# Second attention: the transposes of a pair's probabilities in the middle of the filling chunk, not ahead of it

## The chip, the cores and the metric

The kernel runs on one core of one Trainium2 chip. The metric is the device time of one execution in microseconds (us), the median of several executions. The engines are named as in the profile: PE is TensorE (its matmuls), PEld its weight loads, DVE is VectorE, ACT is ScalarE, POOL is GpSimd, SP issues most of the weight transfers.

## The reference

Two transformer blocks follow each other on 256 tokens of width 1024, in float32. The change lies in the second block, in its two attentions (one with a forget gate, "F", and one with three branches: selected blocks "S", window "W", compressed "C"). Cut to what matters:

```
z = rms_norm(x, norm_mix) @ w_in
y_a = rg_lru_mixer(...)            # recurrence: gelu(gate) * scan
y_b = short_conv_mixer(...)        # three taps
y_c = fox_mixer(...)               # 4 heads: softmax(q k + decay) v           "F"
y_d = nsa_mixer(...)               # 4 heads: g0*softmax_c v + g1*softmax_s v + g2*softmax_w v
mixed = concatenate([rms_norm(y_a), rms_norm(y_b), rms_norm(y_c), rms_norm(y_d)])
x = x + mixed @ w_out
```

That makes 16 jobs (head and branch), each a score, a softmax, a transpose of the probabilities and a product with the values.

## The kernel before

Every engine has an instruction stream written by hand, and they meet in semaphores; nothing is scheduled automatically. A float32 matrix product is made of three matmuls on split operands (`product`, L1949 to L1951: high times high, high times low, low times high). Weights arrive by DMA in `raw`, ACT writes the high part `w_hi` (L719) and DVE the low part `w_lo` (L1246); this runs four panels ahead of PE.

The 16 jobs of the second attention are taken two at a time: pairs 0 to 7, of kinds F, F, S, W, C, S, W, C. For pair x (loop over `PAIRS`, jobs a and b) the streams do this:

- PE: `make_scores` of pair x+1 (L2188 and L2189, for kind C L2185 and L2186); `turn(a)`, `turn(b)`: transposes of pair x's probabilities into banks ps2 and ps3 (L2202, three each, for kind C L2199, two each); for pairs 0 to 6 one chunk of the input projection, `chunk_out`, 8 products of three matmuls, "the filling chunk"; for pair 7 instead `wout_panel(0)`, the first panel of the output projection, as long as a chunk; then `gather(a)`, `gather(b)`: products with the values (L2224 and L2225, for kind C L2218).
- DVE: scores of pair x+1 out of the banks (L1461, L1464), a weight split, sometimes a piece of the recurrence or convolution, then the probabilities of pair x+1, scaled by L1483, which raises `p_ready`. `turn` waits for `p_ready`.
- ACT, in this order: exponentials of job a+2 (L897), `pt_copy(a)` and `pt_copy(b)` (L907, for kind C L905): copies of the transposes to `ptb`, which raise `pt_copied`; exponentials of job b+2; then the copy of the filling chunk (L1070). `pt_copy` waits for the transposes (`pt_done`), `gather` for `pt_copied`.

After pair 7 ACT goes on with the Gelu of the recurrence's gate (L1200, with an activation table load ahead of it), the squares of y_b (L1149), a second table load (L1203), the root of their row sum (L1154) and the squares of y_a (L1149). DVE answers with L1740 (sum of two squares, `y_tot`), the scan L1815, L1818 (`ya_ready`), L1744, L1749 (scaled y) and L1756 (its low part, `y_lo`). PE answers in `y_sums(1)` (L2035) and `y_spread(1)` (L2055). `wout_panel(n)` waits for `y_lo` to reach n+1, so `wout_panel(0)` waits for the first L1756 of `y_low(0)`, which DVE does behind the probabilities of pair 7, and `wout_panel(2)` for the first L1756 of `y_low(1)`. `y_sums(1)` stands between `gather` of pair 7 and `wout_panel(1)`, and waits for `y_tot`.

Of the kernel before, what the change touches and what calls it, by code (L numbers as in the profile page):

```python
# [21 lines left out]
KC = D // P  # L22
# [53 lines left out]
FILL_AT = {0: 3, 1: 4, 2: 5, 3: 6, 4: 7, 5: 8, 6: 9}  # L76
# [56 lines left out]
def build(nc, I, out):  # L133
# [111 lines left out]
    def nth(name, k=0):  # L245
        return order[at[name]] + k

    ctx = ExitStack()
    with ctx:
# [39 lines left out]
        def take(*shape, rows=P, start=None):  # L289

            if start is not None:
                where[0] = start
            n = int(np.prod(shape))
            v = arena[0:rows, where[0]:where[0] + n]
            where[0] += n
            assert where[0] <= ARENA, where
            names = "abcd"[:len(shape)]
            if len(shape) > 1:
                v = v.rearrange("p (%s) -> p %s" % (" ".join(names), " ".join(names)),
                                **dict(zip(names[1:], shape[1:])))  # L300
            return v
# [16 lines left out]
        ang, turns, arg = (take(TT, HALF) for _ in range(3))  # L318
# [83 lines left out]
        def s(name):  # L402
            if name not in S:
                S[name] = sem(name)
            return S[name]
# [91 lines left out]
        L = {}  # L497
# [30 lines left out]
        def lin(l, n=SEQ, a=0):  # L528
            return LIN[l % 2][:, a:a + n]
# [9 lines left out]
        def free_name(l):  # L539
            return "lin_free%d" % (l % 2)  # L540
# [50 lines left out]
        def z_buf(g):  # L591

            return (zs if (g // 2) % 2 != (N1 // 2) % 2 else zb)[:, g % 2, :]

        def turned(g):

            if g % 2 == 0:
                return ps[2][:, 0:FW]
            return ps[3][:, 0:FW] if g >= N1 else ps[6][:, P:P + FW]
# [5 lines left out]
        def hi_lo(m, a, n):  # L605
            return w_hi[:, m % HL, a:a + n], w_lo[:, m % HL, a:a + n]
# [18 lines left out]
        for n, (_, parts) in enumerate(panels):  # L625
            raised[n % RAW] += 16 * (len(parts) if parts else 1)
            raw_count.append(raised[n % RAW])
# [1314 lines left out]
        def _(pe):  # L1942
# [3 lines left out]
            def product(dst, stat, mov, start, stop, shared=False):  # L1946

                kw = {"skip_group_check": True} if shared else {}
                T.matmul(dst, stat[0], mov[0], start=start, stop=False, **kw)  # L1949
                T.matmul(dst, stat[0], mov[1], start=False, stop=False, **kw)  # L1950
                return T.matmul(dst, stat[1], mov[0], start=False, stop=stop, **kw)  # L1951
# [4 lines left out]
            def mxp(c):  # L1956
                return mix_hi[:, c, :], mix_lo[:, c, :]

            def await_split(m, i=0):
                pe.wait_ge(lo_done, m + 1 + i * 6)  # L1960

            def await_bank(l):

                if l >= 2:
                    name, v = freed[l - 2]
                    pe.wait_ge(s(name), v)

            def chunk_out(l, act, fresh=None, order=range(KC), middle=None):


                m = outputs[l]
                await_split(m)
                await_bank(l)
                for n, k in enumerate(order):
                    if fresh is not None:
                        pe.wait_ge(s(fresh[0]), fresh[1] + n + 1)
                    if middle is not None and n == KC // 2:
                        middle()
                    ins = product(lin(l), hi_lo(m, k * P, P), act(k), n == 0, n == KC - 1)
                ins.then_inc(panel_used, 1)  # L1980
# [46 lines left out]
            for b in range(4):  # L2027
                for q in range(4):
                    c, t = 2 * b + q // 2, q % 2
# [22 lines left out]
            def spread(dst, v):  # L2052

                for t in range(TT):
                    ins = T.transpose(dst[:, t * P:(t + 1) * P], v[:, t:t + 1].to_broadcast([P, P]), ident[:, :])  # L2055
                return ins
# [111 lines left out]
            def make_scores(g):  # L2168
                kind, h = ALL[g]
                if g >= 2:  # L2170
                    pe.wait_ge(s("z_ready"), g - 1)
                r = slice(HD * (h % 2), HD * (h % 2) + HD)
                if kind == "A":
                    q, k = aqT[r, h // 2, :], akT[r, h // 2, :]
                elif kind == "M":
                    pe.wait_ge(s("qk_copied"), h + 1)
                    q, k = [qkb[:, 2 * x:2 * x + 2, :].rearrange("p a b -> p (a b)") for x in range(2)]
                elif kind == "F":
                    q, k = fqT[r, h // 2, :], fkT[r, h // 2, :]
                else:  # L2180
                    q = nqT[r, h // 2, :]
                    own, other = kskw[r, :], kskw_x[r, :]
                    k = {"S": (own, other)[h % 2], "W": (other, own)[h % 2], "C": kcT[r, :]}[kind]
                if kind == "C":
                    T.matmul(ps[g % 2][:, 0:NCMP0], q[:, 0:P], k[:, 0:NCMP0], start=True, stop=True)  # L2185
                    ins = T.matmul(ps[g % 2][:, P:P + NCMP], q[:, P:SEQ], k[:, 0:NCMP], start=True, stop=True)  # L2186
                else:
                    T.matmul(ps[g % 2][:, 0:P], q[:, 0:P], k[:, 0:P], start=True, stop=True)  # L2188
                    ins = T.matmul(ps[g % 2][:, P:FW], q[:, P:SEQ], k[:, 0:SEQ], start=True, stop=True)  # L2189
                line(ins, "s_done")  # L2190

            def turn(g):

                pe.wait_ge(s("p_ready"), 2 * (g + 1))
                if g >= 2:
                    pe.wait_ge(s("pt_copied"), g - 1)
                if ALL[g][0] == "C":
                    for t in range(TT):
                        ins = T.transpose(turned(g)[0:NCMP, t * P:(t + 1) * P], zc[:, g % 2, t, 0:NCMP], ident[:, :])  # L2199
                else:  # L2200
                    for b in range(3):
                        ins = T.transpose(turned(g)[:, b * P:(b + 1) * P], z_buf(g)[:, b * P:(b + 1) * P], ident[:, :])  # L2202
                line(ins, "pt_done")
# [29 lines left out]
            for x in range(NP1):  # L2233
                a, b = 2 * x, 2 * x + 1
# [189 lines left out]
            for kv in range(2):  # L2424
                for half in range(2):
                    m = ADA + 2 * kv + half
                    n = direct_of[m]
# [59 lines left out]
            def y_sums(n):  # L2487

                pe.wait_ge(s("y_tot"), n + 1)
                if n >= 1:  # L2490
                    pe.wait_ge(s("y_rms"), n)
                    pe.wait_ge(s("y_ready"), 2)
                line(by_token(YSUM[:, 2 * n:2 * n + 2], sq[:, Y_SQ[n], :]), "y_ss")

            def y_spread(n):

                pe.wait_ge(s("y_inv"), n + 1)
                line(spread(Y_FAC[n], yrms[:, 2 * n:2 * n + 2]), "y_fac")

            def wout_panel(n, middle=None):  # L2500

                m, k = nth("wout", n), Y_ROWS[n]
                await_split(m)
                pe.wait_ge(s("y_lo"), n + 1)
                if n == 0:
                    for l in L["fill"][8:10]:
                        pe.wait_ge(s(free_name(l)), freed[l][1])
                for c in range(KC):
                    if c == KC // 2 and middle is not None:
                        y_spread(middle)  # L2510
                    ins = product(ACC2[c // 2][:, SEQ * (c % 2):SEQ * (c % 2) + SEQ], hi_lo(m, c * P, P), mxp(k),
                                  n == 0 and c % 2 == 0, False, shared=True)
                ins.then_inc(panel_used, 1)
# [19 lines left out]
            for x, (a, b) in enumerate(PAIRS):  # L2533
                if x + 1 < len(PAIRS):
                    if x == 1:
                        pe.wait_ge(s("qk_ready"), 7)
                    for g in (a + 2, b + 2):
                        if ALL[g] == ("S", 1):
                            pe.wait_ge(s("kskw_x_in"), 32)
                        if ALL[g] == ("C", 0):  # L2540
                            pe.wait_ge(s("kc_ready"), 1)
                            pe.wait_ge(s("vc_ready"), 1)
                        make_scores(g)
                turn(a)
                turn(b)
                if x in FILL_AT:
                    chunk_out(L["fill"][FILL_AT[x]], hx)
                if x == len(PAIRS) - 1:
                    wout_panel(0)
                gather(a)  # L2550
                gather(b)
                if x == 3:
                    y_sums(0)
                if x == 5:
                    y_spread(0)
# [53 lines left out]
```

## Time and profile before

| | us |
|---|---|
| median of 3 runs | 751.49 |
| lowest and highest of them | 751.16 and 754.23 |
| the profiled execution | 751.95 |
| its span, first to last instruction | 750.1 |
| PE busy in it | 718.8 (96%) |
| DVE busy in it | 549.2 (73%) |
| ACT busy in it | 448.9 (60%) |
| mean granted clock of PE | 0.995 |

A span is the time between the first and the last instruction of the core; 1.85 us of the profiled execution lie around it. A granted clock of 1.00 is 2.4 GHz, 0.50 is 1.2 GHz. The stretch of the second attention is 485 to 536 us from the span's start.

### The profile page before, as it was taken

Reading aid. Unit: us, or ns where it says so; the run is one execution under the profiler, and the core shown is the slowest. Engines: PE = TensorE matmul, PEld = TensorE weight load, DVE = VectorE, ACT = ScalarE, POOL = GpSimd, SP = SyncE. Lnnn points to the kernel's source line nnn. Section 1 sums busy time; section 2 is a strip of 40 time slices with the busy share of each in tenths; the row PEclk is TensorE's granted clock in tenths of the full one; section 3 lists DMA queues with packets and bytes.
Section 4 is the critical chain, followed back from the end, with each engine's and each line's share of the span. In section 5 each row is a group of like instructions: output and inputs, shape, how many; then the busy total and the mean of one; then the engine's idle time right before and its main releaser. Section 6 shows DMA issues by size and latency. Waiting matters only on the chain.

```text
span 750.1 us, 13966 instructions
## 1 busy us (share of the span) xinstructions
PE 718.8 (96%) x4944; PEld 647.4 (86%) x4944; DVE 549.2 (73%) x1060; ACT 448.9 (60%) x857; POOL 78.1 (10%) x112
## 2 busy tenths in 40 slices
PE   2799999999999999999999999999999999999998
PEld 2699898899999899999999999877898888888886
DVE  4887459898797786666666678887887876776764
ACT  5667466666655655455554577898657554545552
POOL 8003021000356000000000002600000000000000
PEclk9999999999999999999999999999999999999999
DMA  9997798888799367665666748842155865666531
GB/s 289 354 289 239 190 218 255 279 270 261 227 333 261 110 188 212 188 194 169 181 199 185 162 117 210 222 139 91 41 158 169 239 181 174 195 192 192 169 112 57
DMA packets 187237, 148.37 MB, mean 198 GB/s; under 512 B 13681, under 2 KB 171315, under 8 KB 187177
## 3 DMA queue, kind: packets, MB, share of 16 engines
q1 hardware_dynamic: 183296, 143.61, 64.8%
q10 hardware_dynamic: 2232, 3.03, 2.2%
q0 software_dynamic: 1664, 1.15, 0.8%
q8 instruction: 27, 0.44, 0.2%
q14 instruction: 18, 0.14, 0.0%
HBM read 146.44 MB, written 1.36 MB: 197 GB/s over the span
## 4 chain that ended last, share of the span: by engine, by line
PE 83%; DVE 7%; ACT 5%; DMA 2%; issue 2%; POOL 0%; SPq 0%; DVEq 0%; ACTq 0%; POOLq 0%
PE ps L2334 20%; PE ps L1949 15%; PE ps L1951 14%; PE ps L1950 14%; PE ps L2336 10%; DMA raw<-in_w_ada 2%; DVE w_lo L1246 2%; DVE arena L1304 1%; ACT w_hi L719 1%; PE ps L2311 1%; PE ps L1997 1%; PE ps L2224 1%; PE ps L2202 1%; PE ps L2189 1%; PE ps L2188 1%
## 5 line engine op out<-in xcount | busy, mean ns | idle before, releaser
L1246 DVE TENSOR_TENSOR w_lo<-raw,w_hi 128x1024 fp32r<-128x1024 f32 (+3 forms) x223 | 270.6, 1235 | 66.7 <-ACT w_hi L719 65.5
L719 ACT ACTIVATE w_hi<-raw 128x1024 fp32r<-128x1024 f32 (+3 forms) x223 | 226.0, 1038 | 22.3 <-DMA raw<-in_w_in 7.8
L2334 PE MATMUL ps<-h,w_hi 128*128 128x512 f32 x672 | 239.1, 396 | 0.0
L2336 PE MATMUL ps<-h,w_lo 128*128 128x256 f32 x672 | 189.4, 282 | 0.0
L2334 PEld LDWEIGHTS ps<-h,w_hi 128*128 128x128 f32 x672 | 126.3, 188 | 29.5
L1949 PE MATMUL ps<-h,w_hi 128*128 128x256 f32 (+1 forms) x440 | 126.9, 288 | 3.7 <-DVE h L1323 1.9
L2336 PEld LDWEIGHTS ps<-h,w_lo 128*128 128x128 f32 x672 | 126.2, 188 | 1.0
L1951 PE MATMUL ps<-h,w_lo 128*128 128x256 f32 (+1 forms) x440 | 123.6, 281 | 0.0
L1950 PE MATMUL ps<-h,w_hi 128*128 128x256 f32 (+1 forms) x440 | 123.5, 281 | 0.0
L1949 PEld LDWEIGHTS ps<-h,w_hi 128*128 128x128 f32 (+1 forms) x440 | 82.7, 188 | 7.7 <-issue 5.0
L1950 PEld LDWEIGHTS ps<-h,w_hi 128*128 128x128 f32 (+1 forms) x440 | 82.8, 188 | 0.0
L1951 PEld LDWEIGHTS ps<-h,w_lo 128*128 128x128 f32 (+1 forms) x440 | 82.6, 188 | 0.1
L998 ACT ACTIVATE arena<-ps 128x256 f32<-128x256 f32 x44 | 16.8, 382 | 70.4 <-PE ps L2336 69.4
L1949 PE MATMUL ps<-g_hi,w_hi 128*128 128x256 f32 x176 | 49.3, 280 | 0.0
L1950 PE MATMUL ps<-g_lo,w_hi 128*128 128x256 f32 x176 | 49.2, 280 | 0.0
L1951 PE MATMUL ps<-g_hi,w_lo 128*128 128x256 f32 x176 | 49.2, 279 | 0.0
L1949 PE MATMUL ps<-mix_hi,w_hi 128*128 128x256 f32 x160 | 47.2, 295 | 1.2 <-DVE mix_lo L1756 0.6
L1011 ACT ACTIVATE g_hi<-arena 128x256 fp32r<-128x256 f32 x44 | 18.4, 418 | 47.3 <-DVE arena L1608 47.3
L1950 PE MATMUL ps<-mix_lo,w_hi 128*128 128x256 f32 x160 | 45.1, 282 | 0.0
L1951 PE MATMUL ps<-mix_hi,w_lo 128*128 128x256 f32 x160 | 45.1, 282 | 0.0
L1588 DVE TENSOR_TENSOR arena<-arena,ps 128x256 f32<-128x256 f32 x44 | 18.5, 420 | 31.7 <-ACT arena L998 31.6
L1007 ACT ACTIVATE arena<-ps 128x256 f32<-128x256 f32 x44 | 16.9, 384 | 40.6 <-PE ps L2336 40.6
(380 smaller groups left out, 1248.3 us busy)
## 6 DMA issues: line engine op xcount, KB each, us to landing
raw<-in_w_in SPq DMA_DIRECT2D x53, 512.0 KB, 5.7
raw<-in_w_down SPq DMA_DIRECT2D x44, 512.0 KB, 4.3
raw<-in_w_gate_up SPq DMA_DIRECT2D x44, 512.0 KB, 4.5
raw<-in_w_ada SPq DMA_DIRECT2D x32, 512.0 KB, 5.0
raw<-in_w_gate SPq DMA_DIRECT2D x22, 512.0 KB, 4.0
raw<-in_w_up SPq DMA_DIRECT2D x22, 512.0 KB, 5.0
raw<-in_w_ada SPq DMA_DIRECT2D x32, 256.0 KB, 6.7
raw<-in_w_o SPq DMA_DIRECT2D x8, 512.0 KB, 5.2
```

The costliest lines, as they stand in the source:

```text
L719: A(w_hi[:, m % HL, 0:w], raw[:, n % RAW, 0:w], ACT.Copy).then_inc(hi_done, 1)
L998: line(A(g_part[:, j % 2, :], bank_of(f, j)[:, SEQ:512], ACT.Copy), "g_part")
L1007: line(A(u_part[:, j % 2, :], UP[j % 2][:, SEQ:512], ACT.Copy), "u_part")
L1011: line(A(g_hi[:, j % 2, :], hf[:, j % 2, :], ACT.Copy), "g_hi")
L1246: V.tensor_tensor(w_lo[:, m % HL, 0:w], raw[:, n % RAW, 0:w], w_hi[:, m % HL, 0:w].bitcast(f32), sub).then_inc(lo_done, 1)
L1304: ins = stt(out=dst, in0=src, scalar=cond[:, k:k + 1], in1=dst, op0=mult, op1=add)
L1588: line(V.tensor_tensor(g_all[:, j % 2, :], g_part[:, j % 2, :], bank_of(f, j)[:, 0:SEQ], add), "g_sum")
L1949: T.matmul(dst, stat[0], mov[0], start=start, stop=False, **kw)
L1950: T.matmul(dst, stat[0], mov[1], start=False, stop=False, **kw)
L1951: return T.matmul(dst, stat[1], mov[0], start=False, stop=stop, **kw)
L2334: T.matmul(bank[:, :], hi, h2[:, k, :, :].rearrange("p a b -> p (a b)"), start=(k == 0), stop=False, skip_group_check=True)
L2336: ins = T.matmul(bank[:, 0:SEQ], lo, h_hi[:, k, :], start=False, stop=(k == KC - 1), skip_group_check=True)
```

## The change

`wout_panel` and `chunk_out` take a function that is called in the middle of their eight products. The two turns of a pair are handed over to it, for pairs 0 to 6 in the filling chunk and for pair 7 in the first output panel, where they stood ahead of both. Nothing else differs; only PE's order changes.

```diff
-            def wout_panel(n, middle=None):
+            def wout_panel(n, middle=None, between=None):
...
                 for c in range(KC):
                     if c == KC // 2 and middle is not None:
                         y_spread(middle)
+                    if c == KC // 2 and between is not None:
+                        between()
                     ins = product(ACC2[c // 2][:, SEQ * (c % 2):SEQ * (c % 2) + SEQ], hi_lo(m, c * P, P), mxp(k),
                                   n == 0 and c % 2 == 0, False, shared=True)
...
                         make_scores(g)
-                turn(a)
-                turn(b)
+
+                def turns():
+
+                    turn(a)
+                    turn(b)
                 if x in FILL_AT:
-                    chunk_out(L["fill"][FILL_AT[x]], hx)
+                    chunk_out(L["fill"][FILL_AT[x]], hx, middle=turns)
                 if x == len(PAIRS) - 1:
-                    wout_panel(0)
+                    wout_panel(0, between=turns)
                 gather(a)
                 gather(b)
```

PE at pair 1, before: scores of pair 2 into ps0 and ps1, then the transposes of pair 1 (`sq` holds the probabilities), then the chunk (`h2` are the activations). The semaphores on which a row waits stand behind it.

```order
L2188 MATMUL ps0<-arena 128x128 [waits z_ready,qk_ready]
L2189 MATMUL ps0<-arena 128x256
L2188 MATMUL ps1<-arena 128x128 [waits z_ready,kskw_x_in]
L2189 MATMUL ps1<-arena 128x256
L2202 MATMUL ps2<-ident,sq 128x128 [waits pt_copied,p_ready]
L2202 MATMUL ps2<-ident,sq 128x128 x2
L2202 MATMUL ps3<-ident,sq 128x128 [waits pt_copied,p_ready]
L2202 MATMUL ps3<-ident,sq 128x128 x2
L1949 MATMUL ps4<-h2,w_hi 128x256 [waits lru_sig,lo_done]
```

The same place in the changed program:

```order
L2188 MATMUL ps1<-arena 128x128 [waits z_ready,kskw_x_in]
L2189 MATMUL ps1<-arena 128x256
L1949 MATMUL ps4<-h2,w_hi 128x256 [waits lru_sig,lo_done]
...
L2202 MATMUL ps2<-ident,sq 128x128 [waits pt_copied,p_ready]
L2202 MATMUL ps2<-ident,sq 128x128 x2
L2202 MATMUL ps3<-ident,sq 128x128 [waits pt_copied,p_ready]
L2202 MATMUL ps3<-ident,sq 128x128 x2
L1949 MATMUL ps4<-h2,w_hi 128x256
```

Twelve matmuls of the chunk now stand ahead of the six transposes and twelve behind them. Pairs 0 and 2 to 6 look alike.

PE at pair 7, before: the last `gather` of pair 6 into ps7, the transposes of pair 7 (`zc`), the first output panel (24 matmuls from `mix_hi` and `mix_lo`), `gather` of pair 7 and `y_sums(1)`.

```order
L2225 MATMUL ps7<-ptb,arena 64x128
L2199 MATMUL ps2<-ident,zc 15x128 [waits pt_copied,p_ready]
L2199 MATMUL ps2<-ident,zc 15x128
L2199 MATMUL ps3<-ident,zc 15x128 [waits pt_copied,p_ready]
L2199 MATMUL ps3<-ident,zc 15x128
L1949 MATMUL ps0<-mix_hi,w_hi 128x256 [waits lin_free0,lin_free1,y_lo,lo_done]
...
L2218 MATMUL ps7<-ptb,arena 64x256 [waits pt_copied] x2
L2035 MATMUL ps6<-ones,sq 128x1 [waits y_ready,y_rms,y_tot]
```

The same place in the changed program:

```order
L2225 MATMUL ps7<-ptb,arena 64x128
L1949 MATMUL ps0<-mix_hi,w_hi 128x256 [waits lin_free0,lin_free1,y_lo,lo_done]
...
L2199 MATMUL ps2<-ident,zc 15x128 [waits pt_copied,p_ready]
L2199 MATMUL ps2<-ident,zc 15x128
L2199 MATMUL ps3<-ident,zc 15x128 [waits pt_copied,p_ready]
L2199 MATMUL ps3<-ident,zc 15x128
L1949 MATMUL ps4<-mix_hi,w_hi 128x256
...
L2218 MATMUL ps7<-ptb,arena 64x256 [waits pt_copied] x2
```

Here the transposes moved behind a wait for `y_lo` and twelve matmuls. DVE, ACT and SP have the same order in both programs, and so do POOL's instructions of this stretch.

## Rows read from the trace of the kernel before

**Rows 1.** PE's waits over the whole span: total us, times, longest us.

```profile
PE ps L2224 <- ACT ptb L907: 1.4, 1, 1.4
...
PE ps L1949 <- DVE mix_lo L1756: 0.6, 1, 0.6
```

**Rows 2.** Timeline of PE at pair 1: start, duration; idle before and releaser in brackets.

```profile
495.47 1.20 PE L2202 MATMUL ps<-ident,sq 128*128 128x128 f32 x6 [1.24 <-DVE sq L1483]
496.43 0.36 PE L1949 MATMUL ps<-h,w_hi 128*128 128x256 f32 x1
...
499.43 0.66 PE L2224 MATMUL ps<-ptb,arena 128*64 128x256 f32 x4
...
500.24 0.50 PE L2188 MATMUL ps<-arena 64*128 64x128 f32 x4
```

**Rows 3.** Timeline of PE, an earlier chunk that is already cut in the middle.

```profile
476.20 0.39 PE L1949 MATMUL ps<-h,w_hi 128*128 128x256 f32 x1
...
477.72 0.38 PE L2440 MATMUL ps<-ident,arena 128*128 128x128 f32 x2
```

**Rows 4.** Timeline of DVE at pair 1: job b's probabilities.

```profile
495.52 0.55 DVE L1483 TENSOR_SCALAR sq<-sq,small 128x128 f32<-128x128 f32 x2
```

**Rows 5.** Timeline of ACT: the copies to ptb of pairs 0, 1 and 5.

```profile
490.81 0.87 ACT L907 ACTIVATE ptb<-ps 128x384 f32<-128x384 f32 x2
...
497.75 0.85 ACT L907 ACTIVATE ptb<-ps 128x384 f32<-128x384 f32 x2
...
521.39 0.85 ACT L907 ACTIVATE ptb<-ps 128x384 f32<-128x384 f32 x2
```

**Rows 6.** Timeline of PE at pair 7 and the output panels behind it.

```profile
528.24 0.52 PE L2225 MATMUL ps<-ptb,arena 128*64 128x128 f32 x3
529.86 0.39 PE L2199 MATMUL ps<-ident,zc 128*15 128x128 f32 x2 [1.11 <-DVE zc L1483]
530.93 0.59 PE L2199 MATMUL ps<-ident,zc 128*15 128x128 f32 x2 [0.68 <-DVE zc L1483]
531.30 0.55 PE L1949 MATMUL ps<-mix_hi,w_hi 128*128 128x256 f32 x1
...
534.00 0.41 PE L1949 MATMUL ps<-mix_hi,w_hi 128*128 128x256 f32 x1
...
535.69 0.65 PE L2218 MATMUL ps<-ptb,arena 15*64 15x256 f32 x4
...
536.26 0.61 PE L2035 MATMUL ps<-ones,sq 128*128 128x1 f32 x4
...
540.19 0.35 PE L1949 MATMUL ps<-mix_hi,w_hi 128*128 128x256 f32 x1
```

**Rows 7.** Windows: length, busy us (instructions) of PE, PEld, DVE, ACT, POOL; granted clock, DMA.

```profile
495.00:500.00 5.00, 4.42 (x36) 3.92 (x38) 4.75 (x23) 4.86 (x15) 0.00 (x0) 1.00 0.43 123
...
530.80:531.00 0.20, 0.07 (x1) 0.07 (x2) 0.20 (x2) 0.00 (x0) 0.00 (x0) 0.95 1.13 343
...
534.20:534.50 0.30, 0.30 (x4) 0.30 (x3) 0.30 (x1) 0.30 (x2) 0.00 (x0) 0.68 0.00 0
```

**Rows 8.** Timeline of ACT behind pair 7.

```profile
531.56 0.37 ACT L905 ACTIVATE ptb<-ps 15x256 f32<-15x256 f32 x1 [0.90 <-PE ps L2199]
531.95 1.28 ACT L1200 ACT_TABLE_LOAD   x1
533.25 0.63 ACT L1200 ACTIVATE arena<-arena 128x512 f32<-128x512 f32 x1
534.14 0.72 ACT L1149 ACTIVATE sq<-bias 128x256 f32<-128x256 f32 x2 [0.26 <-DVE bias L1808]
```

**Rows 9.** Timeline of DVE behind pair 7.

```profile
530.78 0.76 DVE L1756 TENSOR_TENSOR mix_lo<-bias,mix_hi 128x256 fp32r<-128x256 f32 x2
...
534.89 0.43 DVE L1740 TENSOR_TENSOR sq<-sq 128x256 f32<-128x256 f32 x1 [0.19 <-ACT sq L1149]
...
539.62 0.82 DVE L1756 TENSOR_TENSOR mix_lo<-bias,mix_hi 128x256 fp32r<-128x256 f32 x2
```

## The prediction

> **What bounds the kernel now.** I read the page first: PE is busy for 96% of the span, so a moved instruction can only gain where PE stands idle. PE's waits show how little that is: in and behind the second attention 1.24 us at pair 1's transposes, 1.4 us at pair 5's products with the values, 1.11 and 0.68 us at pair 7's transposes, 0.6 us late in the output projection [rows 1, 2, 6]. The reader is to see two kinds of wait there. Those for DVE L1483 (probabilities not ready) are what a later place for the transposes can cover. The one for ACT L907 is the reverse: the copy of the transposes was late, and later transposes can't help it. Then I read the timelines of PE, DVE and ACT side by side over 485 to 560 us, and the chain of waits through it: up to pair 1 it runs through ACT and DVE, in pairs 2 to 4 through PE, from pair 5 to pair 7 through ACT and DVE again.
>
> **Pair 1, a gain.** PE was done with the last scores at 495.47 − 1.24 = 494.23 and stood there until job a's probabilities came; job b's came at 495.52 + 0.55 = 496.07 [rows 2, 4]. Turns of pair 1 and their waiting held PE until 496.43. Changed, the first half of the chunk fills this. It takes 1.52 us, the length of the half that is cut already [rows 3], so from 494.2 to 495.7; turn(b) can start at 496.2 (0.06 us for the semaphore, and some 0.1 us because pair 0's copy, before at 490.81 [rows 5], comes a little later behind its half chunk); it is over by 496.6 and the second half by 498.1. Before, the gather began at 499.43 [rows 2]. Not all of these 1.3 us are kept: ACT's copies of pair 1 stand behind exponentials that DVE sets, so they stay at 497.75, 0.85 us for the two [rows 5], and 0.1 us of delay: job b's is there at 498.7. So gather(b) starts at about 498.8, takes half of the 0.81 us from 499.43 to 500.24 [rows 2], and the next scores start at 499.2, where they stood at 500.24: **1.05 us earlier**.
>
> **Pairs 0 and 2 to 6, nothing or a little loss.** Work only changes places. Two cut halves of 1.52 us are 3.04, a whole chunk is 3.00 [rows 2, 3]: 0.04 us a pair for the extra change of operands, on the path in pairs 2, 3 and 4 and partly inside other waits: **0.05 us lost** is my value for the three, 0.25 us the other end. The cover for the copies shrinks from a whole chunk to half; two copies take 0.87 us [rows 5], with semaphores some 1.1, so 1.5 us hold them if ACT is free, and in its timeline ACT waits for scores in pairs 2 to 4. If it doesn't hold, each of these pairs loses up to 0.5 us. In pair 5 the wait stays: ACT's course there begins at the end of pair 4's chunk and passes two table loads before it copies at 521.39 [rows 5]. All of that shifts with PE, so the 1.0 us goes through pair 5, and through DVE's queue up to pair 7.
>
> **Pair 7, a loss.** Here the half panel can't fill the wait, as it waits itself: for `y_lo`, which DVE raises behind the same probabilities. The first L1756 ends at about 531.2, some 0.4 us after its start at 530.78 [rows 9]; PE began the panel at 531.30 with the transposes done inside the wait [rows 6]. Changed, all is 1.0 us earlier by pair 1: the panel begins at 530.25. PE then has been idle since 527.8, 2.5 us in one piece. Before it was 2.2 us (528.76 to 530.93) with the first two transposes in between, and the granted clock fell from 1.00 to 0.50, 2.4 to 1.2 GHz, at about 530.95 and rose at about 534.3 [rows 7]. I take the same fall, for 3.3 us. Twelve matmuls of the panel took 534.00 − 531.30 = 2.70 us at 0.50 [rows 6], where a half at 1.00 is 1.52. So the first half ends at 532.95; turn(a) takes 0.37 us as turn(b) did (530.93 to 531.30 [rows 6]); turn(b) starts at 533.3; the second half takes 1.5 us at the full clock and ends at 535.2. Before, the gather began at 535.69 [rows 6]: PE is still 0.5 us ahead.
>
> ACT is not. It copied job b 0.63 us after the start of turn(b), in 0.37 us, and the table load for the Gelu followed at 531.95 [rows 6, 8]. Now that is 533.3 + 0.63 + 0.37 + 0.02 = 534.3, **2.35 us later**. The Gelu ends at 536.2 where it ended at 533.9. The squares behind it had waited 0.26 us for DVE [rows 8], which is done by then, so they and all that hangs on them come 2.1 us later: DVE's sum L1740 ends at 537.4 in place of 535.3 [rows 9]. `y_sums(1)` then starts at 537.4, not at 536.26 [rows 6]: PE, ready for it at 535.75, stands for 1.7 us. The sums and panel 1 take 3.93 us (536.26 to 540.19 [rows 6]), until 541.4; panel 2 needs the first half of `y_low(1)`, before at 539.62 + 0.41 = 540.03 [rows 9], 0.16 us ahead of PE, now at 542.1. PE starts panel 2 at 542.2, **2.0 us later** than before. Behind it DVE and ACT are driven by PE, the wait for mix_lo [rows 1] shifts with them, and the feed-forward part is PE's alone, so nothing gives this back.
>
> Two rules of the Trainium skill bear on this. The delay rests on ACT keeping its order: in rows 8 it idles 0.90 us for L2199 while the Gelu, whose input is there, stands behind. "PSUM — Partial Sum Buffer", Engine vs sequencer instructions, says the same, that ScalarE's and VectorE's queues are strictly first in, first out; without that rule the Gelu would keep its place and the result would be 1.0 us less than before, with it 2.0 more. On the clock, rows 7 give one fall of 3.3 us. "TensorE: Matmul & The Clock Gate", What's actually happening, says that the number of slow matmuls after a pause varies from run to run of one kernel; by the row the first half panel costs 2.70 us, by the page it may cost as little as at the full clock.
>
> **The sum.** −1.05 + 0.05 = −1.0 us up to pair 7, and 3.0 us lost from there to panel 2, make +2.0 us. The profiled execution's own time is 751.95 us (span 750.1), so it would be 753.9; it stands 0.46 us above the median of 751.49, so the forecast for the median is **753.5 us**. A measurement of this kernel tells about 0.5%, 3.8 us, from no change: I forecast a small loss that counts as the same.
>
> **The rivals.**
> - *The clock doesn't fall, or only after the first half panel.* For it: the wait of 1.24 us at pair 1 left it at 1.00 [rows 7]. Against: PE is idle longer here than when it fell. Then the half takes 1.52 us, turn(b) starts at 531.9, the table load comes 1.0, the squares 0.7 and panel 2 0.6 us later: 752.1 us. (This is also what the page on the clock would allow.) Chance 0.13.
> - *The delay at pair 7 is absorbed and pair 1's gain stays* (the other side). The table load is on time if turn(b) starts by 530.93, which decides. For it: at the full clock PE needs no more than `y_lo` by 529.2, a gain ahead of pair 7 of 2.0 us. Against: the gain is 1.0, and DVE's and ACT's work from pair 5 on has no idle that could shrink so far. 750.5 us. Chance 0.10, of it 0.02 for a gain of over 0.5%, which would take three quarters of all waits named above.
> - *Slower: the new wait of 1.7 us ahead of `y_sums(1)`, so soon after the pause of 2.5 us, brings or keeps the clock at 0.50.* Panel 1 at 0.50 takes 2 × (2.70 − 1.52) = 2.3 us more, of which 0.6 lie in the wait for `y_lo`: 755.2 us. Half a panel more at 0.50, 1.2 us, or late copies in pairs 2 to 4, 0.5 us each, take it over 755.25. For it: the clock fell at a like mixture of idle and work [rows 6, 7]. Against: it didn't in pair 1. Chance 0.16.
> - *No effect*, because turns and chunk are the same work: 751.5 us, chance 0.03. Against it, rows 8: copies and Gelu follow the turns directly.
>
> **How the numbers follow.** The forecast has 0.58, with its own range of 752.7 to 754.3 (0.25 us for the cuts, 0.7 us for where the clock rises). With the rivals at 750.5 and 752.1 below and 755.2 above, a range from 750.9 to 755.5 leaves out the gain case and the worst of the clock case, some 0.15. Slower by over 0.5% takes the part of the third rival beyond 755.25, and a median drawn up as the one run of 754.23 before was: 0.12. Faster by over 0.5%: 0.02. Within: 0.86.
>
> **What the profile after would show.** Right: no wait of L2202 at pair 1; the distance from DVE's last L1483 of pair 7 to the table load L1200 grown by about 3.3 us; a new wait of PE at L2035 for L1740 of 1 to 2 us, one of about 0.6 us at L1949 for L1756 at panel 2; a clock of 0.50 over most of the first half of panel 0. Wrong in the loop: waits at L2224 in pairs 2 to 4 of over 0.2 us each. The prediction fails if panel 0 begins well ahead of 530 us, if the clock stays at 1.00, or if L1200 isn't late.

## The result, and the profile after

The changed kernel takes **753.95 us** (median of 20 executions, 752.12 to 755.95) against 751.58 us (median of 20, 750.82 to 754.51) of the kernel before in the same session. The two medians lie 2.4 us apart. The ratio taken from all executions is 1.0027 (that of the medians alone would be 1.0032), 95% interval 1.0017 to 1.0038, so +2.0 us (+1.3 to +2.9): a small loss, within 0.5%. The profiled execution took 754.01 us, its span is 752.1 us, the mean granted clock 0.995 as before.

PE's work is the same. Busy times of the page after:

```profile
PE 719.0 (96%) x4944; PEld 647.7 (86%) x4944; DVE 548.8 (73%) x1060; ACT 448.2 (60%) x857; POOL 76.1 (10%) x112
```

Its waits moved. PE's waits after, over the whole span (total us, times, longest us); the first two answer to [rows 1]:

```profile
PE ps L1949 <- DVE mix_lo L1756: 3.6, 3, 2.5
...
PE ps L2224 <- ACT ptb L907: 1.7, 2, 1.5
...
PE ps L2035 <- DVE sq L1740: 0.7, 1, 0.7
```

Three waits for `mix_lo` stand where there was one of 0.6 us: 2.5 us ahead of panel 0, 0.35 ahead of panel 2, and the old one. The wait of `y_sums(1)` is new. The one for L2202 at pair 1 is gone. L2224 waits twice, 1.5 us in pair 5 (1.4 before) and 0.2 us in pair 1; nowhere in pairs 2 to 4.

Timeline of PE after, pair 1, answering to [rows 2] (start, duration, idle before and releaser). L2485 in the first row is the last work ahead of the pairs; the two programs are the same up to it:

```profile
486.53 1.97 PE L2485 MATMUL ps<-bias,arena 128*128 128x256 f32 x8
...
496.10 1.09 PE L2202 MATMUL ps<-ident,sq 128*128 128x128 f32 x6
...
498.79 0.81 PE L2224 MATMUL ps<-ptb,arena 128*64 128x256 f32 x3 [0.19 <-ACT ptb L907]
...
499.44 0.38 PE L2224 MATMUL ps<-ptb,arena 128*64 128x256 f32 x1
...
499.96 0.50 PE L2188 MATMUL ps<-arena 64*128 64x128 f32 x4
```

The transposes no longer wait. Timeline of PE after, pair 7 and the output panels, answering to [rows 6]:

```profile
531.08 0.36 PE L1949 MATMUL ps<-mix_hi,w_hi 128*128 128x256 f32 x1 [2.55 <-DVE mix_lo L1756]
...
532.92 1.05 PE L2199 MATMUL ps<-ident,zc 128*15 128x128 f32 x4
533.63 0.56 PE L1949 MATMUL ps<-mix_hi,w_hi 128*128 128x256 f32 x1
...
536.08 0.65 PE L2218 MATMUL ps<-ptb,arena 15*64 15x256 f32 x4
...
537.45 0.61 PE L2035 MATMUL ps<-ones,sq 128*128 128x1 f32 x4 [0.72 <-DVE sq L1740]
...
542.09 0.36 PE L1949 MATMUL ps<-mix_hi,w_hi 128*128 128x256 f32 x1 [0.35 <-DVE mix_lo L1756]
```

The waits of 1.11 and 0.68 us at the two turns [rows 6] are one of 2.55 us now, ahead of panel 0; two further ones follow, ahead of `y_sums(1)` and of panel 2. Timeline of ACT after, behind pair 7, answering to [rows 8]:

```profile
533.58 0.80 ACT L905 ACTIVATE ptb<-ps 15x256 f32<-15x256 f32 x2 [4.51 <-PE ps L2199]
534.40 1.28 ACT L1200 ACT_TABLE_LOAD   x1
535.70 0.63 ACT L1200 ACTIVATE arena<-arena 128x512 f32<-128x512 f32 x1
536.23 0.70 ACT L1149 ACTIVATE sq<-bias 128x256 f32<-128x256 f32 x2
```

ACT stands for 4.51 us for the turns, and the Gelu, whose input is there, stands behind. The 0.26 us that the squares had waited for DVE are gone. Granted clock around panel 0, by windows of PE (length, busy us (instructions), clock, DMA share, GB/s), answering to [rows 7]:

```profile
531.50:532.00 0.50, 0.50 (x7) 1.00 0.17 48
532.00:532.50 0.50, 0.50 (x6) 0.64 0.00 0
...
535.50:536.00 0.50, 0.50 (x5) 0.95 0.00 0
```

Here it fell some 1 us after the panel's start (from the third quarter of the first half on) and stood at 0.50 until about 535.5. Before, it fell ahead of the panel's start.

Since L2485 starts at another time in every profile (484.9 to 490.1 us, from code that is the same in all), everything below is told as the **distance from its start**. "End" is the end of the span, at the last instruction. In the profile before it starts at 486.10:

```profile
486.10 1.97 PE L2485 MATMUL ps<-bias,arena 128*128 128x256 f32 x8
```

| distance, us | panel 0 | Gelu's table load | `y_sums(1)` | panel 2 | end |
|---|---|---|---|---|---|
| before | 45.20 | 45.85 | 50.16 | 54.09 | 264.00 |
| after | 44.55 | 47.87 | 50.92 | 55.56 | 265.57 |
| change | −0.65 | +2.02 | +0.76 | +1.47 | +1.57 |

What moves L2485 lies ahead of everything that was changed, and it is a good part of the scatter of the times: over the profiles L2485 moves by 5.2 us, the distance from it to the end by 2.8. Between 80 and 118 us ACT waits for weights. These are its waits in the profile before (total us, times, longest us):

```profile
ACT w_hi L719 <- DMA raw<-in_w_in: 2.4, 2, 2.0
```

And these in that of e1, the run below whose L2485 starts last, at 490.11:

```profile
ACT w_hi L719 <- DMA raw<-in_w_in: 7.4, 3, 5.6
```

In the three profiles with L2485 behind 488.9 (e1, e2, e6) PE then waits for ACT L889 near 115 us for 2.4 to 3.6 us, and the granted clock is 0.50 for some microseconds behind it. In all others, with L2485 at 484.9 to 486.8, this wait is 0.9 to 1.7 us and the clock stays at 1.00 there. The sum of ACT's waits isn't the measure (4.8 us in e12, whose L2485 starts at 485.21); what in the transfers brings the long wait about wasn't followed.

### The profile page after: what moved, and what is told of

It reads as the page before. It is cut to its first block, busy times and chain, and to the rows that moved or that the text cites. A ratio compares the mean times of both kernels' runs of the same rounds, so it can differ in the third digit from the quotient of the medians.

```text
span 752.1 us, 13966 instructions
## 1 busy us (share of the span) xinstructions
PE 719.0 (96%) x4944; PEld 647.7 (86%) x4944; DVE 548.8 (73%) x1060; ACT 448.2 (60%) x857; POOL 76.1 (10%) x112
## 4 chain that ended last, share of the span: by engine, by line
PE 80%; ACT 6%; DVE 5%; DMA 5%; issue 2%; SPq 0%; POOL 0%; ACTq 0%; DVEq 0%; POOLq 0%
PE ps L2334 20%; PE ps L1949 14%; PE ps L1951 13%; PE ps L1950 13%; PE ps L2336 10%; DMA raw<-in_w_in 3%; DMA raw<-in_w_ada 2%; ACT w_hi L719 2%; DVE w_lo L1246 2%; PE ps L2311 1%; PE ps L1997 1%; PE ps L2224 1%; DVE arena L1304 1%; PE ps L2189 1%; PE ps L2202 1%
```

## The experiments

The theory was the one on record: pair 1 gains, pair 7 loses more, through the place of the Gelu behind the copies in ACT's order. The rivals were that the loss comes from the clock alone, from the cuts of the other pairs, or that the half panel ahead of the turns matters in itself. Distances of all profiles, in us, and the times; e1 to e4 ran on one chip, e5 to e8 on a second, e9 to e12 on a third. The clock column names a fall close to the pairs' end. Three programs were profiled twice (before and e9, after and e10, e3 and e11): their distances to panel 0 agree within 0.06 us, those to panel 2 within 0.18, 0.69 and 0.00 us. The 0.69 goes with a fall of the clock in one of the two. From panel 2 to the end all profiles lie within 0.4 us (209.9 to 210.3), so smaller differences at the end say nothing. In e6 the panel begins with the turns, and the distance is theirs.

| | turns in the middle for | panel 0 | table load | `y_sums(1)` | panel 2 | end | clock there | ratio to before, interval |
|---|---|---|---|---|---|---|---|---|
| before | none | 45.20 | 45.85 | 50.16 | 54.09 | 264.00 | falls | |
| e9 before again | none | 45.20 | 45.64 | 49.26 | 53.91 | 264.17 | stays | single execution, 751.65 us |
| after | all | 44.55 | 47.87 | 50.92 | 55.56 | 265.57 | falls | 1.0027 (1.0017 to 1.0038) |
| e10 after again | all | 44.61 | 47.17 | 50.22 | 54.87 | 265.09 | stays | single execution, 752.27 us |
| e1 | pairs 0 to 6 | 44.61 | 45.06 | 48.68 | 53.33 | 263.39 | falls early | 1.0014 (0.9991 to 1.0038) |
| e2 | pair 7 | 45.20 | 48.22 | 51.27 | 55.92 | 265.97 | falls | 1.0054 (1.0029 to 1.0080) |
| e3 | pair 1 | 44.41 | 44.86 | 48.48 | 53.12 | 263.24 | stays | 0.9992 (0.9972 to 1.0012) |
| e8 | pairs 0, 2 to 6 | 45.39 | 45.84 | 50.49 | 54.42 | 264.51 | falls | 1.0008 (0.9998 to 1.0018) |
| e4 | all, Gelu first | 44.67 | 43.28 | 48.74 | 53.38 | 263.57 | falls early | 1.0007 (0.9987 to 1.0028) |
| e7 | pairs 0 to 6, Gelu first | 44.67 | 42.67 | 48.74 | 53.38 | 263.62 | stays | 0.9998 (0.9987 to 1.0010) |
| e5 | all, PE kept busy | 44.57 | 47.08 | 50.13 | 55.65 | 265.98 | falls late | 1.0022 (1.0001 to 1.0042) |
| e6 | all, pair 7 at 0 products | 44.67 | 45.74 | 48.80 | 53.44 | 263.37 | stays | 0.9991 (0.9980 to 1.0003) |
| e12 | all, pair 7 at 2 products | 44.61 | 46.94 | 50.16 | 54.64 | 264.79 | falls | single execution, 751.90 us |
| e11 | pair 1 | 44.41 | 44.86 | 48.47 | 53.12 | 263.19 | stays | 0.9981 (0.9969 to 0.9993) |

**e1, e2, e3, e8: each part of the change alone.** One condition was put in, and only it differs between the four:

```diff
+                inside = x < len(PAIRS) - 1      # e1; e2: x == len(PAIRS) - 1
+                if not inside:                   # e3: x == 1; e8: x not in (1, len(PAIRS) - 1)
+                    turns()
                 if x in FILL_AT:
-                    chunk_out(L["fill"][FILL_AT[x]], hx, middle=turns)
+                    chunk_out(L["fill"][FILL_AT[x]], hx, middle=turns if inside else None)
                 if x == len(PAIRS) - 1:
-                    wout_panel(0, between=turns)
+                    wout_panel(0, between=turns if inside else None)
```

> Turns in the middle for pairs 0 to 6, ahead of the panel for pair 7 as before. My theory (pair 1 gains, pair 7 loses): the distance from PE's L2485 to the start of panel 2, 54.1 us before and 55.6 us after the change, becomes 53.4; the time is 0.65 us under before, 750.9. Rival, every cut chunk costs and pair 7 costs nothing: the distance stays near 55.6 and the time 2 us above before. Rival, it is all in the clock's fall: it falls here as well, 54 to 55.6 at random.

> Turns in the middle for pair 7 alone. My theory: the whole loss and none of the gain, a distance from L2485 to panel 2 of 56.2 us, 2.1 us over before's 54.1, and a time of 753.7; the table load for the Gelu starts 4 us behind DVE's last L1483, where it was 1.1 before. Rival, cut chunks cost: 54.1 to 54.3 us and no change of time.

> Turns in the middle for pair 1 alone. My theory: the same gain as with pairs 0 to 6, a distance of 53.3 to 53.4 us, since the other pairs' turns never waited. Rival, the cover of each pair adds up: only a part of what pairs 0 to 6 give.

> Turns in the middle for pairs 0 and 2 to 6, ahead in pairs 1 and 7: the price of the cuts alone. My theory: a distance of 54.1 to 54.3 us, 0 to 0.2 over before, time 751.6. Rival, cuts or late copies cost 0.5 us a pair: 55 or more.

Timeline of PE in e2, the start of L2485, then panel 0, `y_sums(1)` and panel 2:

```profile
488.93 1.97 PE L2485 MATMUL ps<-bias,arena 128*128 128x256 f32 x8
...
534.13 0.35 PE L1949 MATMUL ps<-mix_hi,w_hi 128*128 128x256 f32 x1 [2.55 <-DVE mix_lo L1756]
...
540.20 0.61 PE L2035 MATMUL ps<-ones,sq 128*128 128x1 f32 x4 [0.47 <-DVE sq L1740]
...
544.85 0.36 PE L1949 MATMUL ps<-mix_hi,w_hi 128*128 128x256 f32 x1 [0.35 <-DVE mix_lo L1756]
```

Pair 7 alone begins panel 0 where before began it (534.13 − 488.93 = 45.20), has the three waits of the changed kernel, and starts panel 2 at 544.85 − 488.93 = 55.92, 1.83 us late. The loss needs nothing of the loop. The time of e2 came out higher than the 2.2 us that were expected, 4.1 us above before (2.2 to 6.0) from 8 executions, twice what its distance gives. On that chip the times of the kernel before alone run from 751.46 to 757.58 us, and e2's profile has the long wait near 115 us; whether that is all of the surplus isn't shown. Timeline of PE in e3, pair 1 and panel 2:

```profile
485.06 1.97 PE L2485 MATMUL ps<-bias,arena 128*128 128x256 f32 x8
...
494.59 1.04 PE L2202 MATMUL ps<-ident,sq 128*128 128x128 f32 x6
...
497.24 0.81 PE L2224 MATMUL ps<-ptb,arena 128*64 128x256 f32 x3 [0.19 <-ACT ptb L907]
...
498.40 0.50 PE L2188 MATMUL ps<-arena 64*128 64x128 f32 x4
...
538.18 0.35 PE L1949 MATMUL ps<-mix_hi,w_hi 128*128 128x256 f32 x1 [0.35 <-DVE mix_lo L1756]
```

Pair 1 alone has the next scores at 498.40 − 485.06 = 13.34, where before has 14.14 (500.24 [rows 2] less 486.10): 0.80 us, and 0.79 of it is still there at panel 0. So the whole gain of the loop is pair 1's; at panel 2 it is 53.12, a little more than the 53.3 to 53.4 expected. e8 starts panel 0 0.19 us later than before, e1 0.20 later than e3: two comparisons give the cuts of the other six pairs the same price. At panel 2 e1 is still 0.21 behind e3, but e8 is 0.33 behind before, over the 0 to 0.2 that were expected. Its clock fell 0.2 us behind the start of panel 0, in the profile before 0.3 us ahead of it, so that part isn't laid to the cuts.

Half of that price lies at pair 1. Timelines of ACT, DVE and PE in e8 from pair 0's copies to pair 1's transposes (L2485 starts at 485.19):

```profile
490.00 0.88 ACT L907 ACTIVATE ptb<-ps 128x384 f32<-128x384 f32 x2
...
491.64 1.05 ACT L719 ACTIVATE w_hi<-raw 128x1024 fp32r<-128x1024 f32 x1
```

```profile
492.72 1.23 DVE L1246 TENSOR_TENSOR w_lo<-raw,w_hi 128x1024 fp32r<-128x1024 f32 x1 [1.39 <-ACT w_hi L719]
...
494.06 0.55 DVE L1483 TENSOR_SCALAR sq<-sq,small 128x128 f32<-128x128 f32 x2
```

```profile
494.66 1.21 PE L2202 MATMUL ps<-ident,sq 128*128 128x128 f32 x6 [1.33 <-DVE sq L1483]
```

Pair 0's copies begin at a distance of 4.81, before at 490.81 − 486.10 = 4.71 [rows 5]. ACT's next weight split follows them in its order, DVE's low part waits for it with the probabilities behind, and PE's wait is 1.33 us in place of 1.24 [rows 2]: 0.10 us from end to end. The rows also point at what makes PE wait at pair 1 at all: DVE idles 1.39 us for a weight split just ahead of the probabilities. Moving that split wasn't tried.

The times of e1 and e3 on the first chip tell neither from no change; e1's profile alone spent 4 us more ahead of L2485, where it is the same program. What is said of e1 and e3 rests on the distances.

**e4, e7: the Gelu ahead of pair 7's copies.** Only ACT's order differs from the changed kernel (e4) or from e1 (e7); line numbers behind it grow by one:

```diff
+                if not more:
+                    line(A(lg, lg, ACT.Gelu_apprx_tanh), "lg_ready")
                 pt_copy(a)
...
-            line(A(lg, lg, ACT.Gelu_apprx_tanh), "lg_ready")
             act.wait_ge(s("yb_ready"), 1)
```

> The changed kernel, and on ACT the Gelu of the recurrence's gate, with its table load, ahead of pair 7's two copies in place of behind them. My theory (the loss is the Gelu's chain held behind the copies): the squares of y_b start 1.8 us earlier than after the change, PE doesn't wait at y_sums(1), panel 2 starts 1.5 us earlier, distance 54.1 and time as before, 751.5. Rival, the loss is PE's own (the slow clock, the half panel and the turns on its path): panel 2 stays at 55.6 us and the time at 753.9.

> Pairs 0 to 6 in the middle, pair 7 ahead of the panel, and the Gelu ahead of pair 7's copies: the version that the theory points to. The squares of y_b then wait for DVE alone; behind pair 7 PE itself is next. Distance 53.3 to 53.4 us, time 750.7 to 750.9, no better than without the Gelu's move by more than 0.2 us. Rival, ACT still bounds there: another 0.5 us or more off.

Timeline of ACT in e4 behind pair 7:

```profile
529.01 1.28 ACT L1178 ACT_TABLE_LOAD   x1
530.31 0.63 ACT L1178 ACTIVATE arena<-arena 128x512 f32<-128x512 f32 x1
...
532.30 0.64 ACT L905 ACTIVATE ptb<-ps 15x256 f32<-15x256 f32 x2 [1.36 <-PE ps L2200]
...
533.23 0.72 ACT L1149 ACTIVATE sq<-bias 128x256 f32<-128x256 f32 x2 [0.29 <-DVE bias L1809]
```

Table load and Gelu now lie inside ACT's wait for the turns, the squares wait for DVE again, PE doesn't wait at `y_sums(1)`, and panel 2 starts at 53.38 in place of 55.56. The turns of pair 7 stand exactly as late in PE's order as in the changed kernel. That is the whole loss, removed by ACT's order alone: expected was panel 2 at 54.1, as before, and the gain of pair 1 shows as well. The time of e4 (1.0007, 0.9987 to 1.0028) fits, but is too wide to show it by itself. In e7, where the turns of pair 7 are on time, the same move brings nothing (53.38 against e1's 53.33). e4's profile left the clock at 1.00 at pair 7, so part of its 2.18 us against the after profile is the clock; against e10, whose clock stayed up as well, it is 1.49 us.

**e5: is it the clock?** Ahead of panel 0 PE waits only until the bank is free and then multiplies constants (`ident` and `ones`) five times, about as long as `y_lo` takes:

```diff
+                    l = L["fill"][8]
+                    pe.wait_ge(s(free_name(l)), freed[l][1])
+                    keep_awake(lin(l), 5)
                     wout_panel(0, between=turns)
```

> The changed kernel with five 128x256 float32 products of constants in PE's pause ahead of panel 0, into a bank that panel 0 starts anew, so their result isn't used. They fill the pause of 2.6 us with about 2.3 us of matmuls. My theory: the granted clock stays at 1.00 through panel 0, turn(b) starts about 0.6 us earlier than after the change, and the distance from L2485 to panel 2 falls only by that, from 55.6 to 55.0. Rival, the slow clock is the loss: it falls to 54 and the time to that of before.

Timeline of PE in e5:

```profile
526.87 2.43 PE L2061 MATMUL ps<-ones,ident 128*128 128x256 f32 x10
529.49 0.36 PE L1949 MATMUL ps<-mix_hi,w_hi 128*128 128x256 f32 x1 [0.19 <-issue]
```

Windows of PE in e5 behind it, around the wait for `y_tot` (535.05 is the start of `y_sums(1)`):

```profile
534.00:535.00 1.00, 0.00 (x0) 1.00 0.00 0
535.00:536.00 1.00, 0.95 (x5) 0.66 0.00 0
536.00:537.00 1.00, 1.00 (x6) 0.50 0.03 8
```

The dummy matmuls took the pause away, and the clock was 1.00 through panel 0: the table load comes 0.79 us earlier than in the changed kernel. (That they kept it there isn't shown; e10 below had 1.00 without them.) But the distance of the load is still 1.23 us above before's, so a full clock doesn't undo the loss. Then the clock fell some 0.3 us behind the next pause, of 1.54 us ahead of `y_sums(1)`. From there to panel 2 it is 5.52 us, where after has 4.64, with the wait for `y_lo` of 0.35 us gone: nothing is left of the gain at panel 2, which starts at 55.65 where 55.0 was expected. This is the third rival's mechanism, at less than its price.

**e6, e12: where the turns of pair 7 stand in the panel.**

```diff
-                    if c == KC // 2 and between is not None:
+                    if c == 0 and between is not None:       # e6; e12: c == 2
                         between()
```

> As the changed kernel, but pair 7's turns stand at the first product of panel 0, behind its wait for y_lo and ahead of its first matmul. My theory: what costs is the half panel between that wait and the turns; without it ACT is 0.3 to 0.5 us late in place of 2.5, distance 53.8 and time 751.3. Rival, the wait for y_lo ahead of the turns costs: distance over 55.

> As the changed kernel, but pair 7's turns behind two of panel 0's eight products, in place of four. If each matmul between the wait for y_lo and the turns is paid by ACT's chain, panel 2 stands between 53.44 us (turns at the start) and 55.56 (in the middle): 54.3 to 54.7. Rival, a threshold such as a fall of the clock: near one of the two ends.

Turns behind 0, 2 and 4 products of the panel put panel 2 at 53.44, 54.64 and 55.56. No free stretch shows between the three: ACT waits for the turns, and the products ahead of them delay it. The clocks of the three differ, so the size of a single step isn't read from them, and e12, within its expected 54.3 to 54.7, doesn't exclude by itself that a fall of the clock places it there. At 1.00, e6 and e10 give 1.43 us at panel 2 for the four products, which took 1.49 us. e6 came out better than expected (53.8, with ACT 0.3 to 0.5 us late against before): its table load is at 45.74, before at 45.85, though 0.68 us behind e1's. e6 is as e1 within 0.11 us, which it should be, as the transposes only follow the wait for `y_lo`.

**e9, e10: both kernels once more, unchanged.**

> The kernel before once more, for a second profile. If distances in the trace from L2485 on are a steady measure, L2485 to panel 2 is again 53.9 to 54.1 us and to the end 263.8 to 264.1, wherever the clock falls; a spread of over 0.5 us would take the readings by distance away.

> The changed kernel once more. Steady: 55.2 to 55.9 us to panel 2, 265.3 to 266.0 to the end. The place at which the clock falls is expected to differ from the first profile of it.

Timeline of PE in e9, `y_sums(1)` and panel 2:

```profile
534.89 0.61 PE L2035 MATMUL ps<-ones,sq 128*128 128x1 f32 x4 [0.43 <-DVE sq L1740]
...
539.54 0.36 PE L1949 MATMUL ps<-mix_hi,w_hi 128*128 128x256 f32 x1 [0.40 <-DVE mix_lo L1756]
```

Timeline of PE in e10, the same and panel 0:

```profile
529.92 0.36 PE L1949 MATMUL ps<-mix_hi,w_hi 128*128 128x256 f32 x1 [2.55 <-DVE mix_lo L1756]
531.41 0.60 PE L2199 MATMUL ps<-ident,zc 128*15 128x128 f32 x4
...
535.53 0.60 PE L2035 MATMUL ps<-ones,sq 128*128 128x1 f32 x4 [1.58 <-DVE sq L1740]
...
540.18 0.36 PE L1949 MATMUL ps<-mix_hi,w_hi 128*128 128x256 f32 x1 [0.35 <-DVE mix_lo L1756]
```

The granted clock was 1.00 in both over all of this. For the kernel before that makes 0.18 us at panel 2 (53.91 against 54.09): the slow panel 0 had only covered waits of 0.43 and 0.40 us, which appear when it is fast. At the end e9 is no earlier at all (264.17 against 264.00). For the changed kernel it makes 0.69 us (54.87 against 55.56). So without any fall the change costs +0.96 us at panel 2 and +0.92 at the end, with one fall each +1.47 and +1.57.

e9 lies in the expected range at panel 2 and 0.07 us over it at the end. e10 misses both of its ranges, 54.87 against 55.2 to 55.9 and 265.09 against 265.3 to 266.0: the distance behind panel 0 isn't steady in the changed kernel, but moves with the clock. The 0.69 us is over the 0.5 us that were set as the mark for the kernel before, above which the distances would be no measure, so no difference under 0.7 us at panel 2 is read here between profiles whose clocks differ from panel 0 on; the 2.18 and 1.49 us of e4 stand.

**e11: the better part once more.** e3, unchanged, on another chip.

> The turns in the middle for pair 1 alone, timed once more, on another chip: it has the shortest distance to the end so far, 263.24 us against 264.00 before. Expected 0.75 us under before, 0.999 of it; a measurement of this kernel may not tell that from 1.000.

750.40 us (median of 11) against 751.44, 1.0 us less: ratio 0.9981, interval 0.9969 to 0.9993, a gain of 1.4 us (0.5 to 2.3). The end lies at 263.19 from L2485, 0.81 us less than in the profile before and 0.98 less than in e9. With e3's 0.9992 (0.9972 to 1.0012), the turns in the middle of pair 1's chunk alone are the version with the shortest distance to the end, by 0.2 us over e1 and e6; it beats the kernel before on one of two chips, by about 1 us.

## Why the prediction was right, and where its terms were off

Forecast 753.5 us, measured 753.95; a forecast loss of 2.0 us, measured 2.0 by the ratio (2.4 between the medians). The mechanism stands: e3 shows the gain, e2 the loss, and e4 that the loss goes through ACT's order. That the size agrees so well is in part luck. By the distances the gain of the loop was 0.35 us too large, the loss at pair 7 0.9 us too large, the sum at panel 2 0.5 us too high, and the times then moved by more than the distances.

Point 1 uses one row more of the profile before, the timeline of PE where the two gathers of pair 1 begin (499.43 to 499.46):

```profile
499.43 0.44 PE L2224 MATMUL ps<-ptb,arena 128*64 128x256 f32 x2
```

1. **Pair 1.** Right: the transposes wait no more, ACT's copies stay (distance 11.74, before 11.65: the 0.1 us of delay that was set down), the gain passes through pair 5 and DVE's queue to pair 7. Off: the gain is 0.71 us at the next scores after, not 1.05. The failing term is "gather(b) starts at about 498.8, takes half of the 0.81 us". Copy b ended at 11.74 + 0.84 = 12.58, as forecast (12.6). Job b's first matmul is the third of the row at 498.79 and ends with it, at 499.60; as long as the first, 0.43 us, it began at 499.17, a distance of 12.64. The next scores began at 499.96 − 486.53 = 13.43. So gather(b) took 0.79 us, not 0.4. The 0.81 us of [rows 2] are for two gathers that run beside each other, each filling 64 of the array's columns. In the row shown above the list, the first matmul of each starts within 0.01 us of the other. Halving that time is wrong as soon as a wait parts them.
2. **Cuts of the other pairs.** 0.05 us was my value for the three, 0.25 the other end; the six cost 0.19 to 0.20 at panel 0. By the next scores of pair 1, e8 has lost 0.10 us, through pair 0's cut: its later copies reach DVE through ACT's next weight split, as the rows of e8 show. That 0.1 us stands in my term for pair 1, not in this one, so it is the other five that cost 0.1 us where 0.05 was set down. Right: no wait of L2224 in pairs 2 to 4, half a chunk holds the copies.
3. **Sum up to pair 7.** Forecast −1.0 us, measured −0.65 at panel 0.
4. **Pair 7, the pause.** One wait of 2.55 us ahead of panel 0, forecast 2.5. Right.
5. **Pair 7, the first half panel.** Forecast 2.70 us at a clock of 0.50; measured 532.92 − 531.08 = 1.84, because the clock fell only some 1 us into it. In e10 it was 531.41 − 529.92 = 1.49 at 1.00. The table load is therefore +2.02 us late (forecast 2.35), and the second half ran at 0.50 in place of the first.
6. **From ACT back to PE.** Right in kind: copies, table load, Gelu, squares, L1740, `y_sums(1)`, then L1756, panel 2; e4 shows that the delay hangs on ACT's order. Smaller in size: `y_sums(1)` waited 0.72 us (1.58 in e10), forecast 1.7, and panel 2 came 1.47 us late, forecast 2.0. Counted from panel 0, L1740 ended 0.83 us sooner than forecast (6.32 against 7.15) and PE got there 0.15 us later (5.65 against 5.5), its second half panel having been slow instead of its first. Counted from panel 0, where the terms of the loop are out, pair 7 costs 1.47 + 0.65 = 2.12 us, not 3.0; in e2 1.83.
7. **To the end.** Nothing gave the delay back: +1.47 us at panel 2, +1.57 at the end. Right.

So the distances give −0.65 + 2.12 + 0.10 = +1.57 us where the sum had +2.0; the span of the profile gives 2.0, since L2485 started 0.43 us later in it, where nothing differs. **The times moved by 2.0 us by the ratio, and the 0.4 us (or 1.1 us, counting without a fall of the clock) between that and the distances aren't settled.** Of the two sets of 20, the lowest executions differ by 1.3 us and the highest by 1.4, near the distances; the medians differ by 2.4. Two reasons are open: the changed kernel has two more pauses behind which the clock can fall, as in e5, and each set has its own share of executions with late weights ahead of L2485. One or two profiles of each kernel can't show how often either happens.

Of the signs on record, these came: no wait of L2202 at pair 1, none of L2224 in pairs 2 to 4, new waits at L2035 and at panel 2. Their sizes were off: 0.72 us in place of 1 to 2, and 0.35 in place of 0.6. From DVE's last L1483 of pair 7 to the table load it is 2.7 us more, not 3.3 (534.40 − 530.28 against 531.95 − 530.51 in the timelines of DVE and ACT), and the clock of 0.50 covered the second half of panel 0 rather than the first. One sign was set too strictly: the prediction was to fail if the clock stayed at 1.00, but in e10 it stayed and the loss was there.

The first rival, no fall of the clock, gave +0.6 us with the forecast gain of 1.0; e10 against e9 is this case, +0.96, the same mechanism with the smaller gain of the loop. The rival that absorbs the delay fails: its condition was a gain of 2.0 us ahead of pair 7. No effect is out, since the interval of the ratio leaves out 1. The third rival's fall behind the second pause was seen in e5 alone, at about 0.9 us between `y_sums(1)` and panel 2 where 1.7 net were set down. "TensorE: Matmul & The Clock Gate" of the Trainium skill, What's actually happening, has the count of slow matmuls at a kernel's start vary from run to run of one kernel. What after and e10 show behind a pause is like it: 2.55 us of pause in both, with a fall in one.

## What to carry to other kernels

An independent instruction that stands behind a dependent one on an in-order engine (here Gelu and its table load behind the copies) turns any delay of the producer into a delay of everything behind it; before moving work later, look at what else is queued behind its consumer, and consider moving that ahead. Filling a wait pays only where the filler isn't itself waiting for the same producer: here pair 1 gained because the chunk was ready, pair 7 lost because the panel wasn't. Apply such a change place by place: of eight places here one cost two microseconds, six cost 0.2 us together, and the one that gained was worth about a microsecond by itself (0.8 us by the distances).

## What the runs showed of the hardware

- Two gathers whose products each fill 64 of the array's columns take 0.81 us issued back to back [rows 2], and one of them 0.79 us alone (after, pair 1): parting them costs nearly a whole one.
- The clock's fall isn't tied to the longest pause. e10 kept 1.00 after pauses of 2.55 and 1.58 us. In e5 it fell some 0.3 us behind a pause of 1.54 us, in the changed kernel 1.1 us behind one of 2.55 us. In e1 it fell while PE was working again, 1.8 us behind pair 5's wait of 1.5 us and long before the pause at pair 7. Windows of PE in e1 there:

```profile
526.00:528.00 2.00, 2.00 (x18) 0.80 0.70 207
528.00:530.00 2.00, 2.00 (x11) 0.50 0.22 64
```

- A fall of the clock at panel 0 cost the kernel before next to nothing (0.18 us at panel 2 against e9, where PE waits 0.43 and 0.40 us for DVE instead); in the changed kernel, where ACT depends on that panel's first half, one cost 0.69 us (against e10). Each is one pair of profiles.
- One wait far ahead can shift all that follows: with PE's wait near 115 us at 0.9 to 1.7 us L2485 starts at 484.9 to 486.8, with 2.4 to 3.6 us (e6, e2, e1) and the fall of the clock behind it at 488.9 to 490.1. Reading distances from a common instruction takes this out.
